# Fourteen low parts of weight chunks in the sparse attention: VectorE in place of GpSimd

## The reference, cut to what matters

```python
q = _rope(_rmsnorm(q, q_norm_g), positions)          # 16 heads of 64
k = _rope(_rmsnorm(k, k_norm_g), positions)          # 4 heads of 64
qi = _rope(qi, positions)                            # 8 index heads of 64
ki = _rope(_layernorm(ki, idx_k_ln_g, idx_k_ln_b)[:, :, None, :], positions)[:, :, 0, :]
s = jnp.einsum('bqhd,bsd->bqhs', qib, ki)
score = jnp.einsum('bqhs,bqh->bqs', jax.nn.relu(s), wib).astype(jnp.float32)
_, sel = lax.top_k(score, topk)                      # 128 keys for each query
...
p = jax.nn.softmax(logits, axis=-1).astype(vg.dtype)
o = jnp.einsum('bqgrk,bqkgd->bqgrd', p, vg)
```

## Time and profile before

| | |
|---|---|
| median of three runs | 2851.05 us |
| the profiled execution | 2849.39 us, span in the profile 2847.6 us |
| granted TensorE clock, mean | 0.972 |
| PE busy | 2756.6 us (97%) |
| PE weight loads busy | 2174.6 us (76%) |
| DVE busy | 1359.3 us (48%) |
| ACT busy | 936.6 us (33%) |
| POOL busy | 813.4 us (29%) |

### The profile page before, as it was taken

The page is one execution under the profiler, slowest core; times in us unless marked ns, Lnnn a source line. Parts: engine busy times, 40 slices in busy tenths (PEclk is TensorE's granted clock), DMA queues, the critical chain, the costliest instruction groups (busy, mean ns, idle before and its releaser), DMA issues.

```text
span 2847.6 us, 30406 instructions
## 1 busy us (share of the span) xinstructions
PE 2756.6 (97%) x12474; PEld 2174.6 (76%) x12474; DVE 1359.3 (48%) x1932; ACT 936.6 (33%) x1528; POOL 813.4 (29%) x683
## 2 busy tenths in 40 slices
PE   7999998999999989999999987999999999999999
PEld 6788886777777768888888654468888888888887
DVE  4343255545665534544424697564333454633323
ACT  4222243333444322432224423443222232332221
POOL 5563024443654487457300233410000000000000
PEclk9999999999999999999999996699999999999999
DMA  5453243333333255344433211022333423333332
GB/s 168 141 148 121 97 114 107 101 95 87 110 104 104 82 144 163 115 134 148 119 126 101 62 45 44 9 67 67 96 97 133 126 59 96 126 97 96 96 111 82
DMA packets 380765, 294.52 MB, mean 103 GB/s; under 512 B 14805, under 2 KB 334545, under 8 KB 380625
## 3 DMA queue, kind: packets, MB, share of 16 engines
q1 hardware_dynamic: 363632, 240.33, 28.4%
q0 software_dynamic: 16992, 52.25, 6.1%
HBM read 290.40 MB, written 2.13 MB: 103 GB/s over the span
## 4 chain that ended last, share of the span: by engine, by line
PE 84%; DVE 9%; ACT 3%; POOL 2%; DMA 1%; issue 1%; SPq 0%; DVEq 0%; ACTq 0%; POOLq 0%
PE PS L342 17%; PE PS L343 16%; PE PS L345 14%; PE PS L408 7%; PE PS L410 7%; PE PS L409 7%; PE PS L347 2%; PE PS L839 2%; PE PS L379 1%; PE PS L380 1%; PE PS L381 1%; PE PS L860 1%; DVE SCW L2076 1%; DVE M L2073 1%; PE PS L849 1%; DVE WL L1474 1%
## 5 line engine op out<-in xcount | busy, mean ns | idle before, releaser
L342 PE MATMUL PS<-HH,WH 128*128 128x512 f32 x2248 | 906.6, 403 | 0.0
L343 PE MATMUL PS<-HL,WH 128*128 128x512 f32 x2248 | 878.6, 391 | 0.0
L345 PE MATMUL PS<-HH,WL 128*128 128x512 f32 x1967 | 769.7, 391 | 0.0
L1474 DVE TENSOR_TENSOR WL<-RAW,WH 128x1024 fp32r<-128x1024 f32 (+1 forms) x306 | 400.9, 1312 | 546.1 <-ACT WH L899 545.9
L342 PEld LDWEIGHTS PS<-HH,WH 128*128 128x128 f32 x2248 | 424.6, 189 | 131.2 <-issue 47.5
L343 PEld LDWEIGHTS PS<-HL,WH 128*128 128x128 f32 x2248 | 424.5, 189 | 90.8 <-issue 6.8
L899 ACT ACTIVATE WH<-RAW 128x1024 fp32r<-128x1024 f32 (+1 forms) x318 | 330.5, 1041 | 377.4 <-PE PS L347 312.5
L345 PEld LDWEIGHTS PS<-HH,WL 128*128 128x128 f32 x1967 | 371.0, 189 | 79.4
L2248 POOL TENSOR_SCALAR ADA<-ADA,CA 128x512 f32<-128x512 f32 x168 | 294.7, 1754 | 12.5 <-DMA ADA<-in_ada_w 5.0
L2245 POOL TENSOR_TENSOR ASUM<-ASUM,ADA 128x512 f32<-128x512 f32 x168 | 230.4, 1372 | 14.0
L1474 DVE TENSOR_TENSOR WLr<-RAWD,WHr 128x1024 fp32r<-128x1024 f32 x82 | 101.7, 1240 | 257.4 <-ACT WHr L899 257.4
(11 more groups left out here) (327 smaller groups left out, 3468.4 us busy)
## 6 DMA issues: line engine op xcount, KB each, us to landing
ADA<-in_ada_w POOLq DMA_DIRECT2D x192, 256.0 KB, 3.2
RAW<-in_ffn_w_gate SPq DMA_DIRECT2D x88, 512.0 KB, 3.9
RAW<-in_ffn_w_up SPq DMA_DIRECT2D x88, 512.0 KB, 3.9
RAWD<-in_ffn_w_down SPq DMA_DIRECT2D x88, 512.0 KB, 3.4
RAW<-in_w_in SPq DMA_DIRECT2D x84, 512.0 KB, 3.9
RAW<-in_conv_w_in SPq DMA_DIRECT2D x24, 512.0 KB, 3.9
RAW<-in_attn_w_in SPq DMA_DIRECT2D x16, 512.0 KB, 3.8
RAW<-in_w_mlstm_branch SPq DMA_DIRECT2D x8, 512.0 KB, 4.0
```

Of the source, the lines that this page charges most:

```text
L342: pe.matmul(PS[:, b, :], wh[:, k, :], hi[:, k, :], start=k == 0, stop=False)
L343: pe.matmul(PS[:, b, :], wh[:, k, :], lo[:, k, :], start=False, stop=False)
L345: pe.matmul(PS[:, b, :], wl[:, k, :], hi[:, k, :], start=False, stop=False)
L1474: return v.tensor_tensor(out, x, y, op).then_inc(*tick("dve", *event))
```

## The change

The fourteen low parts leave GpSimd, and VectorE makes them, as it makes those of all other chunks. The instruction is the same, a `tensor_tensor` subtraction of 128 x 1024 numbers. On VectorE it stands where `lows(i + 2)` is called, ahead of the four steps of the chunk.

```diff
-ON_POOL = range(DSA + 5, DOUT + 2)
...
@@ VectorE, lows
             at_i["split"] += 1
-            if j in ON_POOL:
-                continue
             w.wait_ge(*at("hi", j))
             tt(weight_part(m, "WL", j), raw_part(m, j), weight_part(m, "WH", j).bitcast(F32), ALU.subtract, "lo", j)
@@ GpSimd
-    at_i.update(chunk=DSA + 3, split=DSA + 5, slow=False)
+    at_i.update(chunk=DSA + 3, slow=False)
     plan = m["plan"]
-
-    def lows(upto):
-        while at_i["split"] <= upto:
-            j = at_i["split"]
-            at_i["split"] += 1
-            if j in ON_POOL:
-                w.wait_ge(*at("hi", j))
-                tt(weight_part(m, "WL", j), raw_part(m, j), weight_part(m, "WH", j).bitcast(F32), ALU.subtract, "lo", j)

     def fm():
         i = at_i["chunk"]
         at_i["chunk"] += 1
-        lows(i + 2)
```

## The result

| | before | after |
|---|---|---|
| median | 2850.84 us (13 executions) | 2857.05 us (13 executions) |
| ratio, 95% interval | | 1.0023 [1.0014, 1.0033] |
| profiled execution, span | 2849.39, 2847.6 us | 2858.08, 2856.2 us |
| granted TensorE clock, mean | 0.972 | 0.971 |

The changed kernel is 6.2 us slower. One of its executions took 7148.56 us and is left out of the ratio; why it took so long is not known.

What follows compares the result with a forecast made beforehand. VectorE's queue was taken to bound about 1630 to 1770 us, TensorE the time before and after. Added 15.1, given back 7.1, new holds 0.4: 8.4 us on 2851.05 gives 2859.5 us, range 2853 to 2868.

Steps and rivals of the forecast that it cites:

- 246: Low part behind 245, ahead of work TensorE waits for at 1590.31: between 0 and 2.5 us added, taken as 1.0.
- 254: Low part near 1665.7 us: VectorE waits 1.2 for ScalarE's high part and works 1.26, 2.5 us added.
- 259: Low part at 1721.36, ahead of block 3's search: wait 2.4, work 1.26, 3.7 us added, covered by nothing.
- holds at 1647.44 and the scan: VectorE instructions at 1647.44 and 1649.30, stretched by GpSimd's low part: 1.5 and at least 0.7 us given back.
- hold at 1675.64: VectorE instruction of 2.48 us against 0.29 at rest, held by GpSimd's low part: 2.2 us given back.
- the pocket, with 258 in it: About 1710 to 1721 us, where VectorE waits for TensorE at its lower clock: the low part of 258 adds 0.
- Ready in time: Low parts of 255, 256, 257: ScalarE's high parts ready when VectorE comes, so no wait, 3.8 us added in all.
- Runs alike outside the stage: Up to the first of these chunks and from the output projection on, both traces run alike, only shifted.
- The cheap one: Rival for the stage: 246 hidden, extra holds absent, scan hold larger, wait at 254 shrinking; 5.5 us slower, 2856.5; chance 0.27.
- The holds are worth more than the work: Rival: each low part on GpSimd held VectorE's path for 2.39 us; 11 us faster, 2840; 0.10 with the earlier clock.
- The clock that returns earlier: Rival in the attention: TensorE's full clock returns before 1825.38; each 20 us worth at most 10; 0.10 with the holds rival.
- the clock that returns later in B: Rival in the attention: clock returns some 8 us later, 4 us more, 2863 to 2864; 0.15 including late loads or low parts.

Runs made afterwards that it cites:

- the repeat: The changed kernel run again with nothing changed, against the kernel before: 2857.64 against 2848.39 us, ratio 1.0034.
- the third profile of the change: The changed kernel run once more with nothing changed, a single execution: 2858.20 us, beside 2848.39 for the kernel before.
- the first four experiments: Kernel before with only some low parts on VectorE: all but 259, 2854.96 us; only 259, 2852.77; only 246 to 250, 2847.80; only 251 to 257, 2850.82.

## Why the prediction was right, step by step

It said 2859.5, that is 8.4 us slower. Measured were 6.2 us at first and 9.3 in the repeat (2857.64 against 2848.39), and 7.3 to 10.3 in A. The two profiled executions differ by 8.6 in span, next to 8.4, and that is luck: it is 5.44 + 10.31 - 7.03, of which the last and most of the first come from the execution. The ledger, from the third profile of the change against the kernel before (differences of the starts of the same instructions, counted from the start of the stage):

| step | predicted | measured |
|---|---|---|
| 246 | 1.0 | 1.03 |
| 251 | 1.6 | 1.60 |
| 252, 253 | 2.5 | 0.99 + 1.06 |
| 254 | 2.5 | 2.41 |
| 255 to 257 | 3.8 | 3 x 1.13 |
| 259 | 3.7 | 3.73 |
| holds at 1647.44 and the scan | -2.2 | -2.44 |
| holds at 1667.34, 1669.90 | -2.7 | -1.84 - 0.88 |
| hold at 1675.64 | -2.2 | -2.18 |
| new holds | +0.4 | 0 |
| other waits, ahead of 255 above all | 0 | +0.8 |
| the pocket, with 258 in it | 0 | -0.3 |
| sum | 8.4 | 7.3 |

- *Work.* I took 1.26 for each low part. Behind a wait it is 1.25; where it waits for nothing it pushes the next instruction back by only 1.06 to 1.14, since it overlaps what stands before it: in the changed kernel that of 252 starts at 1652.82 while the replace before it runs to 1652.90. (The 0.99 of 252 also holds 0.13 from a small hold that went.) Five such terms make 0.9 of the 1.1 us between sum and ledger; the rest are the smaller differences of the other rows, which nearly cancel.
- *Waits.* 1.2 ahead of 254 and 2.4 ahead of 259 were 1.25 and 2.50 (2.49). I had explained them by the order of ScalarE's instructions, and each came in every version that has that low part there. "Ready in time" was wrong for 255 in the repeats: there VectorE waits 0.48 us for its high part, in the first profile not at all. Ahead of that wait, between 90 and 99 us of the stage, the clock was low for 6.8 us in the repeats and for 3.4 in the first profile, and not at all in the kernel before. No run separates the two, but with all of 246 to 255 on VectorE the wait came in the three profiles with 6.8 us and in neither of the two with 3.4. The third profile, and the kernel before at the same place of the stage:

```profile
1672.00:1676.00 4.00, 4.00 (x9) 2.29 (x8) 3.59 (x7) 0.00 (x0) 0.00 (x0) 0.50 0.40 131
```
```profile
1670.00:1674.00 4.00, 4.00 (x18) 3.15 (x18) 3.77 (x6) 1.21 (x3) 0.93 (x1) 1.00 0.42 131
```

- *Chunk 246.* The two low parts 245 and 246 took 3.44 us together instead of 2.45, since GpSimd multiplied by the cosine in that time (1591.12, 1.26 us). My estimate of 1.0 between 0 and 2.5 was right, but the delay fades to 0.64 where TensorE has work. It comes back at the low part of 251, where ScalarE's high part is as late and VectorE waits 0.76 instead of 0.32; the ledger counts that under 246.
- *Holds.* They came back as reckoned. The scan falls to 0.69 (I had only a bound from 0.96), the sum of 1675.64 to 0.29. The Trainium skill (SBUF — State Buffer, "Who interferes with whom") says that a VectorE instruction with two inputs in SBUF, or one in a two-port mode, and a GpSimd instruction that reads SBUF shut each other out, and that one with at most one such input outside those modes does not contend. The traces agree, in the 3.44 us above and in the searches of blocks 1 and 2, whose `max` took 0.43 and 0.56 us throughout the kernel before and whose replace 0.41 and 0.54 to 0.55, though GpSimd's low parts ran beside some of them.
- *TensorE's idle times.* Those at the first score were to grow from 5.11 to 8 or 9: 8.30 and 8.80. That at 1705.81 was to grow from 3.81 by 2 or 3, and this was wrong: it fell to 3.00. The delay is there (the score comes 4.70 us late relative to the start), but TensorE spent part of it idle earlier (0.94 us at 1595.25 are new, and 1.29 at 1675.28 stand for 0.19), and part of it busy, at a clock that was low for 3.4 us more just behind either place. A delay can be spread over more rows, and over slower work, and doesn't have to show in the row of the wait.
- *Runs alike outside the stage.* Wrong for the first profile: 5.44 us were lost ahead of it. Part of that is the granted clock, with the same code: it is low for 51.2 us ahead of the stage against 44.4, among them 0.92 against 1.00 from 980 to 1000 us. 6.8 us more at half speed are worth 3.4. The other 2 us are not explained, and in the stretch from 1040 to 1080 us both clocks average 0.91.

From the stretches of both kernels, the changed one first:

```profile
980.00:1000.00 20.00, 19.08 (x72) 12.82 (x73) 7.57 (x18) 6.20 (x9) 7.63 (x7) 0.92 0.28 70
...
1040.00:1080.00 40.00, 34.84 (x141) 27.00 (x140) 12.45 (x13) 7.92 (x10) 33.29 (x26) 0.91 0.50 145
```
```profile
980.00:1000.00 20.00, 19.54 (x83) 13.97 (x82) 7.91 (x17) 6.75 (x10) 9.76 (x9) 1.00 0.35 103
...
1040.00:1080.00 40.00, 34.84 (x143) 27.01 (x142) 13.47 (x13) 9.46 (x12) 32.96 (x28) 0.91 0.51 148
```

- *The rivals.* The cheap one (5.5 us) lies below what A shows; the times alone would not exclude it, since both intervals, 4.0 to 9.4 us and in the repeat 4.3 to 15.1, hold it as well as 8.4. "The holds are worth more than the work" is wrong for the fourteen together and right for four of them. The clock that returns earlier did happen in one profile (B 141.37), but in none of the repeats; the clock that returns later in B didn't happen at all. Why A scatters from 167.1 to 170.1 can be read from the clock. The dip at the start of the stage, worth 1.6 us, is in the first and second profile of the change and not in the third. In the pocket the low clock lasted 13.6 us in the first profile, worth 2.2, and 10.2 in the repeats as before. Against that the first profile lacks the 0.8 of other waits.
- *The signs of being wrong.* The wait ahead of 259 was there, and TensorE waited for no low part in any of the three profiles. The third sign, another clock between 1770 and 1830, did show in the first profile, and only the repeats told that it was the execution's.

**What stays open.** Of the 31 executions of the kernel before beside the first four experiments seven took 2831 to 2835 us, and those have a mean granted clock of 0.978 or 0.979, where the ones near 2850 have 0.970 to 0.972. The low share of the time is twice what is missing to 1.00: 0.044 against 0.056 of 2850 us, 34 us less at half speed, which is worth 17 us and so the whole difference. The nearest that the change has to it is one of its ten repeats (2845.12 us at 0.976); beside these, the kernel before had three of thirteen at 0.976 to 0.979, 2833.18 to 2840.48 us. No profile caught one. Where in the program the clock stays up then, and whether the change makes it rarer, was not settled.

## What to carry to other kernels

Price an instruction that is moved to another engine at its place, not at its kind: here fourteen equal subtractions cost between nothing and 3.7 us each, by whether something covers them and whether they wait for a producer. Count the holds between VectorE and GpSimd only where a held instruction is on the path, and expect that a shift of one or two microseconds between the two engines makes or breaks one (0.9 us on VectorE against 2.6 on GpSimd broke the one of 2.2). When an effect of a few us is spread over a stage, measure the stage between two marks of the same instruction and repeat the profile: the rest of the program, unchanged, moved by 5.4 and 7.0 us in one execution, and the time of one profiled pair looked right by luck.

## What I had not expected of the hardware

Between two profiles of the same program the stretches of low clock in this stage agreed to 0.1 us relative to its start (80.2 to 87.0, 128.0 to 138.2, 155.2 to 250.8), while another program's three profiles had three patterns (the last low stretch 160.7 to 249.4, 160.1 to 259.1 and 158.6 to 257.6). And the last low stretch lasts 89 to 99 us in every run, though TensorE was busy for 20.00 of 20 us from 1800 to 1820 within it, at 0.50. In the attention a busy engine in the rows was no sign of the higher clock.
